# Modulation vectors as row sums on VectorE, with a weight ring of three slots, in a two-block transformer kernel

## What is computed

```python
hl = modulate(rmsnorm(xl, norm_w[1]), sh2l, sc2l)      # h * (1 + scale) + shift
xl = xl + 0.5 * g1l * swiglu(modulate(rmsnorm(xl, norm_w[0]), sh1l, sc1l), w_ffn1_in, w_ffn1_out)
mod_l = (jax.nn.silu(c) @ w_mod[l] + b_mod[l])[:, None, :]
```

## Time and profile before

| | |
|---|---|
| median of 3 runs | 2404.45 us (2401.0 to 2405.03) |
| profiled execution, span from its first to its last instruction | 2403.5 us |
| PE busy | 2273.8 us (95%) |
| DVE busy | 1193.6 us (50%) |
| ACT busy | 873.1 us (36%) |
| side unit products on PE (L488) | 99.2 us, 1536 records |
| DMA | 340.16 MB, mean 142 GB/s |

### The profile page before, as it was taken

How to read it: one execution, slowest core, us unless ns; L and a number is a source line. 1 busy time by engine, 2 the same in 40 slices (tenths; PEclk the granted TensorE clock), 3 DMA queues, 4 the chain that set the end, 5 groups by cost and what they waited for, 6 DMA issues and landing times.

```text
span 2403.5 us, 32118 instructions
## 1 busy us (share of the span) xinstructions
PE 2273.8 (95%) x12948; PEld 1859.8 (77%) x12948; DVE 1193.6 (50%) x2086; ACT 873.1 (36%) x1438; POOL 133.6 (6%) x104
## 2 busy tenths in 40 slices
PE   6999999998999999999999999999997997779998
PEld 4777777874677777777777788579996876678888
DVE  3433333647663332335333236776545766647984
ACT  4322222424452222234222225355444364442233
POOL 1000000014000000000000000410011000010001
PEclk9999999999999999999999999999997998889999
DMA  6444454320134444544444433324552221023443
GB/s 271 174 183 175 176 193 173 126 88 18 53 123 193 158 193 158 211 158 158 193 158 193 158 107 116 123 90 175 182 200 92 91 102 70 1 71 132 149 142 138
DMA packets 48457, 340.16 MB, mean 142 GB/s; under 512 B 5184, under 2 KB 7232, under 8 KB 7616
## 3 DMA queue, kind: packets, MB, share of 16 engines
q1 hardware_dynamic: 47136, 336.46, 37.1%
q10 hardware_dynamic: 1184, 1.74, 0.2%
HBM read 337.13 MB, written 1.05 MB: 141 GB/s over the span
## 4 chain that ended last, share of the span: by engine, by line
PE 86%; DVE 7%; ACT 3%; issue 2%; DMA 1%; POOL 0%; SPq 0%; ACTq 0%; DVEq 0%; POOLq 0%
PE bank L516 43%; PE bank L524 21%; PE bank L1001 6%; PE bank L488 4%; PE bank L590 3%; PE bank L601 1%; DMA raw<-stream 1%; PE bank L845 1%; ACT w_hi L1051 1%; DVE w_lo L1520 1%; PE bank L803 1%; DVE h L2001 1%; PE bank L823 1%; PE bank L800 1%; DVE small L1857 1%
## 5 line engine op out<-in xcount | busy, mean ns | idle before, releaser
L1520 DVE TENSOR_TENSOR w_lo<-raw,w_hi 128x1024 fp32r<-128x1024 f32 (+1 forms) x389 | 469.0, 1206 | 922.1 <-ACT w_hi L1051 921.5
L1051 ACT ACTIVATE w_hi<-raw 128x1024 fp32r<-128x1024 f32 (+1 forms) x389 | 403.4, 1037 | 1077.4 <-PE bank L516 1013.6
L516 PE MATMUL bank<-hidden_hi,w_hi 128*128 128x512 f32 (+1 forms) x1392 | 495.8, 365 | 2.5 <-ACT w_hi L1051 2.5
L516 PE MATMUL bank<-hidden_lo,w_hi 128*128 128x512 f32 (+1 forms) x1392 | 492.4, 363 | 0.0
L516 PE MATMUL bank<-h_hi,w_hi 128*128 128x512 f32 (+1 forms) x1416 | 463.1, 344 | 6.2 <-ACT w_hi L1051 4.8
L516 PE MATMUL bank<-h_lo,w_hi 128*128 128x512 f32 (+1 forms) x1416 | 459.4, 341 | 0.0
L524 PE MATMUL bank<-hidden_hi,w_lo 128*128 128x512 f32 (+1 forms) x1392 | 308.7, 363 | 1.9 <-DVE w_lo L1520 1.9
L516 PEld LDWEIGHTS bank<-hidden_hi,w_hi 128*128 128x128 f32 x1392 | 263.3, 189 | 55.2 <-issue 15.6
L516 PEld LDWEIGHTS bank<-h_hi,w_hi 128*128 128x128 f32 x1416 | 269.5, 190 | 43.2 <-issue 7.8
L516 PEld LDWEIGHTS bank<-hidden_lo,w_hi 128*128 128x128 f32 x1392 | 263.4, 189 | 39.7
L516 PEld LDWEIGHTS bank<-h_lo,w_hi 128*128 128x128 f32 x1416 | 269.6, 190 | 29.9 <-issue 0.5
(11 more groups left out here) (271 smaller groups left out, 2080.7 us busy)
## 6 DMA issues: line engine op xcount, KB each, us to landing
raw<-stream SPq DMA_DIRECT2D x317, 1024.0 KB, 4.9
x<-x_in SPq DMA_DIRECT2D x1, 2048.0 KB, 10.0
x<-ctx_in ACTq DMA_DIRECT2D x1, 1024.0 KB, 7.0
out<-x SPq DMA_DIRECT2D x2, 512.0 KB, 3.0
consts<-consts_in ACTq DMA_DIRECT2D x1, 672.0 KB, 7.9
consts<-consts_in SPq DMA_DIRECT2D x1, 464.5 KB, 4.7
params<-params_in SPq DMA_DIRECT2D x1, 413.5 KB, 3.3
```

What stands on the lines that cost most here:

```text
L516: last = nc.tensor.matmul(acc, w_hi[:, buffer, kc, :], v(first_chunk + kc), start=start and kc == n == 0, stop=False)
L1051: nc.scalar.activation(w_hi[:, buffer, 0:chunks, :], raw[at % RING][:, 0:chunks, sub * P:(sub + 1) * P], ACT.Copy)\
L1520: nc.vector.tensor_tensor(w_lo[:, buffer, 0:chunks, :], raw[at % RING][:, 0:chunks, sub * P:(sub + 1) * P], w_hi[:, buffer, 0:chunks, :].b ...
```

## The change

The 88 side units behind the first norm's eight leave the stream. Their weights come as 176 columns instead: column j of `ada0`, `ada1` or `mod` is 128 output features by 1024 inputs, 512 KB, in a ring of two buffers of its own (`columns_raw`). The silu of the two condition vectors, the same in every partition, stands in `cond_rows` (128 x 2 x 1024), loaded and passed through ACT once for the first block's pair and once for the second's. DVE makes one `tensor_tensor_reduce` of 128 x 1024 for each of the two vectors: product, sum along the row, start value the bias, result straight in `mods`. Each waits for the one before it. Where columns stand in DVE's order is `COLUMN_STEPS`: at the end of a step, two a step in up parts, one a step in the first 18 steps of down parts, five in the first mixer's input projection, six in "21". SP issues a step's column DMAs right behind that step's unit. The weight ring has three slots in place of four, the loop on SP is written out, and the late constants, which share their buffer with `cond_rows`, are loaded after the last first-block norm. `rms` and `scaled` now lie in one tensor, `scratch`, that also takes the products of the row sums.

```diff
-RING = 4
+RING = 3
+COLUMN_RING = 2
...
+def _column_steps():
+
+    steps = {}
+    for name, first in (("10", 3), ("20", 2), ("11", 2)):
+        for p in range(first, UP):
+            steps[f"up{name}", p] = 1 if p == 2 else 2
+        for n in range(18):
+            steps[f"down{name}", n] = 1
+    for n in range(4, 9):
+        steps["in0", n] = 1
+    steps["up11", COND_STEP - 2], steps["up11", COND_STEP - 1], steps["up11", COND_STEP] = 1, 0, 0
+    for p in range(3, 9):
+        steps["up21", p] = 1
+    return steps
...
+def _columns_behind():
+
+    behind, n = {}, 0
+    for unit in ORDER:
+        of, j = unit
+        counts = [COLUMN_STEPS.get((of, j), 0)] if of.startswith("up") else \
+            [COLUMN_STEPS.get((of, 2 * j + sub), 0) for sub in range(2)]
+        behind[AT[unit]] = list(range(n, n + sum(counts)))
+        n += sum(counts)
...
-            for s in range(RING):
-                sp.dma_start(raw[s][:, :, :], stream[s]).then_inc(unit_full[s], 16)
-            with sp.Fori(1, n_rounds) as i:
-                for s in range(RING):
-
-                    sp.wait_ge(unit_begun, i * RING + (s + 2 - RING))
-                    sp.dma_start(raw[s][:, :, :], stream[i * RING + s]).then_inc(unit_full[s], 16)
-            for n in range(n_rounds * RING, n_units):
-                sp.wait_ge(unit_begun, n + 2 - RING)
+            for n in range(n_units):
+                if n >= RING:
+                    sp.wait_ge(unit_begun, n + 2 - RING)
                 sp.dma_start(raw[n % RING][:, :, :], stream[n]).then_inc(unit_full[n % RING], 16)
+                if n == AT["up10", 1]:
+                    sp.dma_start(late[:, 0:2 * D], cond_in[0]).then_inc(loaded, 16)
+                if n == AT["up11", COND_STEP - 1]:
+                    sp.wait_ge(column_done, 2 * FIRST_MOD)
+                    sp.dma_start(late[:, 0:2 * D], cond_in[1]).then_inc(loaded, 16)
+                for c in COLUMNS_BEHIND[n]:
+                    if c >= COLUMN_RING:
+                        sp.wait_ge(column_done, 2 * (c - COLUMN_RING + 1))
+                    sp.dma_start(columns_raw[c % COLUMN_RING][:, :], columns_in[c]).then_inc(column_full[c % COLUMN_RING], 16)
...
@@ pe: swiglu, down
-                    if side_before(at):
-                        side_sum(at - 2)
-                        side_sum(at - 1)
...
-                            if gv == 0 and batch_ended(at) is not None:
-                                side_turn(batch_ended(at))
...
@@ act
+            def cond_silu(b):
+
+                act.wait_ge(loaded, 48 + 16 * (b + 1))
+                nc.scalar.activation(late[:, 0:2 * D], late[:, 0:2 * D], ACT.Silu).then_inc(sem("cond_rows"), 1)
...
-                    if batch_ended(at) is not None:
-                        side(batch_ended(at))
+                    if (name, p) in (("10", 2), ("11", COND_STEP)):
+                        cond_silu(int(name == "11"))
...
+                act.wait_ge(column_done, 2 * len(COLUMNS))
+                act.dma_start(late[:, 0:N_CONSTS - EARLY_CONSTS], consts_in[:, EARLY_CONSTS:]).then_inc(sem("late_consts"), 16)
...
@@ dve
+            def column(n):
+
+
+                name, j = COLUMNS[n]
+                dve.wait_ge(sem("cond_rows"), 2 if n >= FIRST_MOD else 1)
+                dve.wait_ge(column_full[n % COLUMN_RING], 16 * (n // COLUMN_RING + 1))
+                bias = param("b_mod" if name == "mod" else f"b_{name}", j, 1)
+                for c in range(2):
+                    if n:
+                        dve.wait_ge(column_done, 2 * (n - 1) + c + 1)
+                    nc.vector.tensor_tensor_reduce(column_products[c], columns_raw[n % COLUMN_RING][:, :], cond_rows[:, c, :], 1.0, bias,
+                                                   ALU.mult, ALU.add, mods[list(SIDES).index(name)][:, j, c:c + 1])\
+                        .then_inc(column_done, 1)
...
@@ dve: swiglu, step p
                     rest(p - 1, (p - 1) % PAIRS)
+                    columns(f"up{name}", p)
...
@@ dve: down, step n
                         raw_low(norm_after, 2 * (older // 2 // len(GROUPS)) + older % 2)
+                    columns(f"down{name}", n)
```

More of the change, by code:

```diff
@@ L100, in _order @@
             name = f"{n}{i}"
-            with_up, with_down = SWIGLU[name]
             for p in range(UP):
                 order += [next(sides)] if p == 1 and name == "10" else []
-                order += [next(sides), next(sides)] if 2 <= p <= with_up and p % 2 == 0 else []
                 order.append((f"up{name}", p))
-            for j in range(4 * len(GROUPS)):
-                order += [next(sides), next(sides)] if j < with_down and j % 2 == 0 else []
-                order.append((f"down{name}", j))
+            order += [(f"down{name}", j) for j in range(4 * len(GROUPS))]
             if n == 1:
@@ L119 @@
 N_UNITS = len(ORDER)
[L122 to L144, removed]
+def _columns_behind():
[6 more added lines that the diff above has]
+        n += sum(counts)
+    assert n == len(COLUMNS) and COLUMNS[sum(len(behind[at]) for at in range(AT["up11", COND_STEP]))] == ("mod", 0)
+    return behind
+COLUMNS_BEHIND = _columns_behind()
 PROJECTIONS = {
@@ L201, in const @@
             first, width = CONSTS[name]
-            return consts[0:rows, first + a:first + a + (width - a if n is None else n)]
+            held, first = (consts, first) if first < EARLY_CONSTS else (late, first - EARLY_CONSTS)
+            return held[0:rows, first + a:first + a + (width - a if n is None else n)]
         ident, ones = const("ident"), const("ones")
         unit_full = [sem(f"unit_full{s}") for s in range(RING)]
+        column_full = [sem(f"column_full{s}") for s in range(COLUMN_RING)]
+        column_done = sem("column_done")
         unit_begun = sem("unit_begun")
@@ L1200, in down @@
                 for n in range(2 * 4 * len(GROUPS)):
-                    j, sub = n // 2, n % 2
-                    if sub == 0 and batch_ended(AT[f"down{name}", j]) is not None:
-                        side(batch_ended(AT[f"down{name}", j]))
                     if n + 1 < 2 * 4 * len(GROUPS):
@@ L1483, in _ @@
             act.wait_ge(sem("cond_zero"), 1)
[L1484 to L1487 removed]
+            nc.scalar.activation(cond[:, :, CENTRE:CENTRE + 2], param("c1").rearrange("p (k c) -> p k c", c=2), ACT.Silu)\
+                .then_inc(sem("cond_ready"), 1)
             for j in range(KC):
@@ L1512, in _ @@
             class At:
-                half, batches = 0, 0
+                half, batches, columns = 0, 0, 0
             def convert(at, sub, chunks=KC):
@@ L1526, in side @@
                 dve.wait_ge(sem("side_turned"), b + 1)
-                turned = bank[TURN_BANK][:, 0:4 * BATCH_MAX].rearrange("p (q n c) -> p n q c", q=2, c=2)
-                for which, name in enumerate(SIDES):
-                    mine = [(pos, j) for pos, (of, j) in enumerate(BATCHES[b]) if of == name]
-                    if not mine:
-                        continue
-                    (pos, j), n = mine[0], len(mine)
-                    first = PARAMS[("b_ada0", "b_ada1", "b_mod")[which]][0] + 2 * j
-                    bias = params[:, first:first + 2 * n].rearrange("p (n q) -> p n q", q=2).unsqueeze(3).broadcast_to([P, n, 2, 2])
-                    last = nc.vector.tensor_tensor(mods[which][:, 2 * j:2 * (j + n), :].rearrange("p (n q) c -> p n q c", q=2),
-                                                   turned[:, pos:pos + n], bias, ALU.add)
-                    if (name, j + n - 1) != BATCHES[b][-1]:
-                        own.mark(last)
@@ L1539, in side @@
-                own.wait(own.n)
-                last.then_inc(sem("side_done"), 1)
-                At.batches = b + 1
+                name, j = BATCHES[b][0]
+                n = len(BATCHES[b])
+                turned = bank[TURN_BANK][:, 0:64].rearrange("p (q n c) -> p n q c", q=2, c=2)[:, 0:n]
+                bias = param("b_ada0", 2 * j, 2 * n).rearrange("p (n q) -> p n q", q=2).unsqueeze(3).broadcast_to([P, n, 2, 2])
+                nc.vector.tensor_tensor(mods[0][:, 2 * j:2 * (j + n), :].rearrange("p (n q) c -> p n q c", q=2),
+                                        turned, bias, ALU.add).then_inc(sem("side_done"), 1)
@@ new lines, in side, with columns @@
+                At.batches = b + 1
+            def columns(stage, step):
+                for _ in range(COLUMN_STEPS.get((stage, step), 0)):
+                    column(At.columns)
+                    At.columns += 1
+            def column(n):
[9 more added lines that the diff above has]
+                        .then_inc(column_done, 1)
@@ L1543, in factors, with modulated_by @@
+            def modulated_by(which, first, n):
+                name = list(SIDES)[which]
+                dve.wait_ge(sem("side_done"), At.batches)
+                if (name, first + n - 1) in COLUMN_AT:
+                    assert At.columns > COLUMN_AT[name, first + n - 1]
```

(9 more changed lines are left out.)

78 lines of the change are left out of this document (39 added, 39 removed).

## The result

The changed kernel takes **2570.65 us** (median of 4 runs, 2564.18 to 2574.91) against 2404.68 of the kernel before in the same comparison: ratio 1.0694, 95% interval 1.0677 to 1.0712, slower. The forecast was 2567.0 in a range of 2450 to 2680.

The account below looks back on a forecast made before the run. The prediction took PE to bound the kernel before, and a closed wait through SP's queue the changed one: up parts 108, down parts 53, small ones 3, sum +164 on 2403.5, giving 2567 us, range 2450 to 2680.

Parts of the forecast that it names:

- The loop: SP's queue: next unit issued only after the previous landed, was converted and DVE did four sums; floor of 14.3 us a step.
- Rival A: Issue order doesn't bind and columns hide in DVE's free time, so 91.5 us go: 2312 us; chance 0.06.
- The turn: Up-part round trip of converts, four sums, SP's wake and transfer: 14.3 us, between 12.6 and 18.5; PE needs 10.88.
- the up parts: Up parts of "10", "20", "11": +38.7, +42, +27, together +108 us, with slack in the first round.
- the small terms: Columns in in0 and up21 cost +3 us, from 0 to 8; other small items nothing.
- Price of a row sum: Each 128x1024 sum on DVE taken at 1.26 us, from L1520's 1.23 plus 0.03; scan rate would give 2.3.
- Rival B: Row sums run at the scan's rate, 2.3 us each, up round 18.5 us: 2840 us; chance 0.08.
- Down parts: Nine units a part wait for columns, two run at PE's pace: +14.9, +14.9 and +23.2, together +53 us.
- The two long rounds: Down parts, n=6 and 7: raw_low waits for ACT's raw_high, then columns and transfer follow: 17.0 us each.
- Ring of three: Weight ring with three slots: units still asked for two ahead, covered by PE's time, so it costs nothing.
- What the profile was to show: If right: beat about 14.3 us, w_hi's transfer idle some 200 us, SP waiting for sums, PE below 90%, DVE near 1.6 ms.
- rival C: PE's 3.4 us gaps hold its clock at 1.2 GHz, unit 21.8 us, sign clock digits below 9: 2920 us; chance 0.03.

Follow-up runs that it names:

- e1: Changed kernel with SP issuing a step's columns behind the next weight unit, same transfers, sums and slots: 2314.5 us, ratio 0.9637 to the kernel before.
- e3: Changed kernel with a step's row sums placed ahead of the next half's convert on DVE, SP's order kept: 2316.72 us, ratio 0.9645 to the kernel before.
- e4: Changed kernel with each row sum over the first 128 of 1024 elements, transfers and waits kept: 2359.74 us.
- e5: Changed kernel with each column's transfer cut from 512 KB to 64 KB, sums at full width, waits kept: 2477.27 us.
- e6: Changed kernel with only a step's second column issued behind the next weight unit: 2346.17 us, ratio 0.9752 to the kernel before.
- e7: Changed kernel with each row sum made twice, SP's issue order kept: 2928.14 us.
- e2: Kernel before with a weight ring of three slots in place of four, nothing else: 2710.05 us.
- e8: Changed kernel with each row sum made twice and the columns issued behind the next weight unit: 2570.44 us.

## Why the prediction was right

**The loop was seen, and it is the cause.** "Unit p+1 can't be asked for until unit p has landed, been converted, and DVE has done four sums" is the chain above, edge by edge. e1 and e3 cut two different edges and each gives 2315 to 2317; e4, e5, e6 and e7 lengthen or shorten it and the beat follows. Rival A's number, 2312, was what the change would do without the loop, and e1 measures it as 2314.5 (span 2309.0).

**The turn, term by term.** The forecast was 14.3, the trace says 14.55. Sums: 1.26 each forecast, 1.205 apart measured (4.82 for four, not 5.04). SP's issue to landing: 6.35 forecast from one column in front, 6.75 measured with a second one 2.4 us ahead of it; in e6, with one close in front, the column's issue to w_hi takes 6.04 (164.10 to 170.14) where it takes 6.77 here. The last sum's tail of 0.08 (1.28 long, 1.205 apart) was not in the forecast. The rest, 0.02 + 1.09 + 1.15 + 0.60, is as read from rows 6 within 0.01, and SP follows the last sum by 0.04. So the errors of the terms, -0.22, +0.40 and +0.08, cancel in part. Averaged over the up parts, the turns on ACT take 14.51 us in "10" and 14.27 in "20" (17 each), and 14.46 in "11" (11).

**That the total came within 1 us is luck.** On the forecast's own cut the up parts are 13 us above it and the down parts 13 below, and these two errors cancel. Of the up parts' 13 us, 10 lie in the units before the full beat. The forecast gave them slack ("PE finds the next unit 1 us early, the second stalls it 2.3 us"); from w_hi to w_hi, units 2 to 5 of "10" take 49.8 us where it had 45.8, units 2 to 4 of "20" 37.8 where it had 34.9. Of the small terms, the +3 for in0 and up21 stands against 3.5 in the two mixers and 0 in up21, and the start's +3.5 and the end's -3.1 were not forecast.

**Price of a row sum.** It was taken from L1520 against the scan's rate; the timeline of DVE:

```profile
160.81 1.28 DVE L1559 CUSTOM_DVE_ANT_0 scratch<-columns_raw,late,params 128x1024 f32<-128x1024 f32 x1
162.01 0.08 DVE L1559 DVE_READ_ACCUMULATOR2_ANT mod_ada<- 128x1 f32 x1
162.01 1.28 DVE L1559 CUSTOM_DVE_ANT_0 scratch<-columns_raw,late,params 128x1024 f32<-128x1024 f32 x1
```

A sum of two fp32 SBUF operands takes 1.28 us, and the read of the accumulator lies beside the next one. Rival B falls. The Trainium skill's rule of half throughput, which its page gives for an STT (Vector Engine (DVE) Microarchitecture Reference, "Points that are easy to get wrong"), does not show in this instruction, which takes 1.28 us and not 2.2; its statement that a stage reading its own result has no bubble (DVE: opcode table, instruction layouts, handler registers and perf-mode slots, "Datapath and trigger behaviour") agrees with 1.28.

**Down parts: +39.8 against +53, one step wrong.** The forecast let nine units wait, the last of them 12.0. But the down part's columns end with step 17, so nothing of DVE stands between unit 9 and the issue of unit 10: that step took 7.22 in "10" and "20" and 8.77 in "11", 12.8 us less than forecast in the three together. The rest is small: the other eight rounds of a part are 2.0 shorter over all three, the last two units take 20.4 a part and not 19.1 (+3.9), and the parts of the kernel before were 2.3 longer than the forecast took them to be. The two long rounds were about as worked out, 17.0 forecast against 17.58 in "10" and, here from the chain of waits, 413.08 - 395.99 = 17.09:

```profile
395.99 0.03 ACT w_hi L1062
...
404.30 1.20 DVE scratch L1559
...
406.74 0.33 SPq L474
...
407.11 5.95 DMA raw<-stream
413.08 0.85 ACT w_hi L1062
```

A column's sums still follow the raw_low that waited, and only behind them does SP get to the unit: the order that the forecast had given.

**Ring of three: "nothing" was wrong by 3.5 us at the start.** By the wait (`n + 2 - RING`) four slots ask for unit n once unit n-3 has begun, and not n-2 as said above; three slots ask once n-2 has. The cover named was PE's time in the units after; a side unit gives only 1 us of it. In the kernel after PE waits there for a side unit asked for at 29.93 us, from the chain of waits:

```profile
29.93 4.66 DMA raw<-stream
```

The first w_hi comes behind it, at 39.1 us. It comes at 38.2 to 41.9 in the nine profiles with three slots and at 35.65 in the one with four, so by these the cost lies between 2.6 and 6.2 us. After the start the cover holds only because the side pairs are gone, which e2 shows at 304 us; the forecast did not say that.

**What the profile was to show.** Beat 14.3 (14.55), PE below 90% (88%), DVE near 1.6 ms (1611), SP waiting for row sums (1107 us in all): right. "ACT's w_hi idle ended by the raw transfer for some 200 us": 841. I had counted the stall of a turn, but the profile counts all idle time that an event ends, some 10 us a turn (841.3 in 83 waits).

**The clock, rival C.** In the turn above the clock fell after the gap and came back within the turn (windows; columns as in e8's):

```profile
159.90:163.00 3.10, 3.10 (x9) 2.38 (x8) 3.10 (x5) 1.39 (x2) 0.00 (x0) 0.51 0.00 0
163.60:170.00 6.40, 6.40 (x30) 5.26 (x29) 3.85 (x6) 0.00 (x0) 0.00 (x0) 1.00 0.75 260
```

0.51 is the 1.2 GHz level. It does not happen in every turn. The turn above with its two neighbours:

```profile
143.49:157.97 14.48, 11.14 (x48) 8.93 (x48) 8.39 (x12) 3.12 (x4) 0.00 (x0) 1.00 0.43 146
157.97:172.52 14.55, 12.79 (x48) 10.08 (x48) 8.39 (x12) 3.12 (x4) 0.00 (x0) 0.88 0.40 144
172.52:187.07 14.55, 11.16 (x48) 8.93 (x48) 8.38 (x12) 3.12 (x4) 0.00 (x0) 1.00 0.42 144
```

PE had stood still for 2.70, 3.34 and 1.75 us ahead of the first matmuls of these three turns. The slow matmuls of the middle one filled part of the gap that followed them, so the turns are of the same length with and without a slow stretch: it cost nothing here, as the rival's own sentence had it. The Trainium skill's account of a kernel that goes cold in every wait (TensorE: Matmul & The Clock Gate, "HAM oscillation — how this bites in real kernels") agrees with the 0.51 but not with the full clock of the two other turns. The sign that the prediction drew from it, clock digits below 9 in the up parts, did not show: the page's digits in "10" are all 9, and the mean clock over that part is 0.94.

## What to carry to other kernels

A queue that prefetches in order must not hold, between two prefetches, a wait on work that itself comes after the first of them: that closes a loop, its pace is the round trip (here 14.55 us), and free time on every engine is no help. Write the loop down as a sum of durations and compare it with the bound engine's step, before looking at busy shares. To open it, move the waiting issue behind one more prefetch, which here turned 2570.65 into 2314.5 us with the same bytes, sums and slots; when it can't be moved, move the work that it waits for ahead of the wait on the prefetched thing (e3).

## What the runs showed of the hardware that was not expected

- The clock: after a gap of 3.34 us PE ran at the 1.2 GHz level for a part of the turn (0.51 from 159.90 to 163.00) at no cost in time; in the turn before, after 2.70 us, and the turn after, after 1.75, the clock was 1.00. In e2, where PE is what everything waits for, such a fall costs 2 us a pair on top of the 4.87 us wait.
- Transfers queued ahead of a 1 MB unit add to its landing, the more the closer they are: 4.9 us in the median behind 64 KB columns, 6.3 behind 512 KB columns 2.4 us apart, 6.8 with both asked for at once.
- A row sum of 128x1024 takes 1.28 us, near the 1.23 of a plain two-operand instruction of that width, and costs 1.205 a piece in a row of four though each waits for the one before.

A third buffer for the columns was not tried.
